# Window steps first with the compressed cells beside them, selected steps after: a hybrid trunk's sparse attention layer

## What is computed

```python
q = rms_norm(q) ; gate = sigmoid(gate)             # 3 gates per head
ck = rms_norm(compress(kc)) ; cv = compress(vc)    # 63 compressed cells per group
for each block of 128 queries:
    # 1. compressed: 63 cells
    s = q @ ck.T * scale + bias ; s = where(valid_c, s, NEG_INF)
    p_c = softmax(s) * any(valid_c) ; o_c = p_c @ cv
    # 2. selected: 8 of 16 blocks of 64 keys, chosen per group by the summed p_c
    imp = sum_over_heads(p_c) @ ov
    idx = top_k(where(valid & forced, FORCE_SCORE, where(valid, imp, -1)), 8)
    o_s = softmax(q @ k_sel.T * scale + bias) @ v_sel
    # 3. window: the last 512 keys
    o_w = softmax(q @ k_win.T * scale + bias + mask) @ v_win
o = gate0 * o_c + gate1 * o_s + gate2 * o_w
```

## Time and profile before

| | us |
|---|---|
| median of 3 runs | 2625.72 |
| lowest, highest | 2622.18, 2634.36 |
| the profiled execution | 2626.59 |
| its span (first to last instruction) | 2624.8 |
| TensorE busy in it | 2527.2 (96%) |
| VectorE, GpSimd, ScalarE busy | 1785.7, 1174.9, 1124.4 |
| mean granted TensorE clock | 0.979 |

### The profile page before, as it was taken

How to read it: one execution, slowest core, us unless ns; L and a number is a source line. 1 busy time by engine, 2 the same in 40 slices (tenths; PEclk the granted TensorE clock), 3 DMA queues, 4 the chain that set the end, 5 groups by cost and what they waited for, 6 DMA issues and landing times. The chain is left out here.

```text
span 2624.8 us, 37850 instructions
## 1 busy us (share of the span) xinstructions
PE 2527.2 (96%) x14000; PEld 2049.3 (78%) x14000; DVE 1785.7 (68%) x2826; ACT 1124.4 (43%) x2184; POOL 1174.9 (45%) x889
## 2 busy tenths in 40 slices
PE   8999889999999999999988999999999999999999
PEld 5777667888887878887876688888788888777887
DVE  6554755477678999853059567666546767899993
ACT  4626544253334434323135566666524333433431
POOL 5362666234445444442236444444633444444441
PEclk8999999999999999999987899999999999999999
DMA  4010003224343544230342423222132334354531
GB/s 168 33 49 33 1 1 117 93 81 161 140 169 134 188 170 146 83 127 32 102 118 65 129 59 100 54 54 54 56 125 79 146 135 170 109 209 149 175 125 65
DMA packets 90973, 275.76 MB, mean 105 GB/s; under 512 B 9879, under 2 KB 38935, under 8 KB 76135
## 3 DMA queue, kind: packets, MB, share of 16 engines
q1 hardware_dynamic: 87240, 255.18, 28.4%
q10 hardware_dynamic: 3552, 18.18, 1.8%
HBM read 197.50 MB, written 73.86 MB: 103 GB/s over the span
## 5 line engine op out<-in xcount | busy, mean ns | idle before, releaser
L1582 PE MATMUL ps<-U_hi,RH 128*128 128x512 f32 x912 | 356.7, 391 | 12.5 <-DVE H L905 4.8
L1586 PE MATMUL ps<-U_lo,RH 128*128 128x512 f32 x912 | 355.7, 390 | 0.0
L1587 PE MATMUL ps<-U_hi,RL 128*128 128x512 f32 x912 | 355.6, 390 | 0.0
L1040 POOL TENSOR_TENSOR RL<-RAW,RH 128x512 fp32r<-128x512 f32 x112 | 156.2, 1395 | 395.2 <-ACT RH L744 395.2
L744 ACT ACTIVATE RH<-RAW 128x512 fp32r<-128x512 f32 x280 | 175.5, 628 | 292.8 <-PE ps L1587 285.4
L1533 POOL TENSOR_SCALAR PX<-PX,rinv,GATE 128x640 f32<-128x640 f32 (+7 forms) x256 | 197.8, 783 | 209.0 <-DVE rinv L3303 209.0
L1582 PE MATMUL ps<-U_hi,W_hi 128*128 128x512 f32 (+2 forms) x656 | 261.9, 399 | 13.3 <-DVE U_lo L2805 10.7
L1582 PE MATMUL ps<-SH,RH 128*128 128x512 f32 x656 | 256.8, 392 | 8.2 <-DVE H L905 4.1
L1586 PE MATMUL ps<-U_lo,W_hi 128*128 128x512 f32 (+2 forms) x656 | 258.2, 394 | 0.0
L1587 PE MATMUL ps<-U_hi,W_lo 128*128 128x512 f32 (+2 forms) x656 | 258.1, 393 | 0.0
L1586 PE MATMUL ps<-SL,RH 128*128 128x512 f32 x656 | 255.9, 390 | 0.0
(11 more groups left out here) (390 smaller groups left out, 6005.9 us busy)
## 6 DMA issues: line engine op xcount, KB each, us to landing
W_raw<-in_pieces SPq DMA_DIRECT2D x30, 1024.0 KB, 5.1
RAW<-in_pieces SPq DMA_DIRECT2D x28, 1024.0 KB, 4.9
RAW<-in_pieces SPq DMA_DIRECT2D x56, 512.0 KB, 7.7
hid_d<-HOA SPq DMA_DIRECT2D x24, 1024.0 KB, 3.9
hid_d<-HOB SPq DMA_DIRECT2D x24, 768.0 KB, 5.4
RHA<-hid_d SPq DMA_DIRECT2D x12, 1024.0 KB, 5.1
RHB<-hid_d SPq DMA_DIRECT2D x12, 768.0 KB, 6.6
U_rawh<-hid_d SPq DMA_DIRECT2D x12, 768.0 KB, 4.8
```

The costliest lines, as they stand in the source:

```text
L1040: G_.tensor_tensor(ring(RL[i], n), quarter(n, (B22, B11)[i - 5]), ring(RH[i], n).bitcast(F32), ALU.subtract).then_inc(u_lop.sem, 1)
L1582: m = mm(o, a_hi, b_hi, start=first, stop=False, skip_group_check=again)
L1586: mm(o, a_hi, b_lo, start=False, stop=False, skip_group_check=again)
L1587: return mm(o, a_lo, b_hi, start=False, stop=last, skip_group_check=again)
```

## The change

Window and selected steps are no longer interleaved: `unit` gives all 64 window steps (eight pairs of eight) first, then all 64 selected ones. The cells' stage is gone as a stage. A cell is now half a pair (both heads, four query blocks), there are 16, and `cell(s, lag)` gives the cell whose part of that lag is due in step s: cell c has its scores at the end of step 4c + 4, maximum 1 step later, exponentials 2, sum 3, `share` 4, clamp, `add_up` and `gate_p` 5, its two turns 6 and 7 (ahead of the value products on TensorE, copied out ahead of the exponentials on ScalarE), its value product and output 9. Queries of pair p are turned in steps 8p - 6 and 8p - 5. The sums of group g are turned in step 32g + 41, chosen over the next six and the mask turned in 32g + 48 and 49.

Window scores are made of three products of 64 rows per head, straight from the pair's turned queries (one head in rows 0 to 63, the other in 64 to 127), the two heads alternating instruction by instruction. The selected ones are as before, with queries read back from memory.

Everything that TensorE turns (probabilities, queries, late keys, cells' scores, cells' probabilities, cells' value products, sums, masks) goes through banks 4 and 5 alternately by one list, `SEQ`; `room` waits until the last but one entry is emptied. GpSimd's two memsets of the mask rows come in steps 50 and 66, its splits of output weights in the last eight steps. The first engine queues are rewritten: window keys are turned first, and the last four key turns lie between the first two window scores and the loop. Loads and stores on SP follow the new order, and some tiles lie at other addresses.

The diff, cut to the order of the work, the banks, the window scores and the cells:

```diff
         SEL, WIN = 0, 1
-        STEPS = [x for k in range(NT) for x in ((SEL, NT - 1 - k), (WIN, NT - 1 - k))]
-        N_S = len(STEPS)
-        N_U = 2 * N_S
-        N_STEP = NH // 2 * N_S
+        N_PAIR = NH // 2
+        N_BR = N_PAIR * NT
+        N_STEP = 2 * N_BR
         N_ALL = 2 * N_STEP
+        N_CELL = 2 * N_PAIR
+        N_CHOOSE = 4 + 2 * NT
 
         def unit(U):
 
-            br, i = STEPS[U // 2 % N_S]
+            s = U // 2
+            br, i = (WIN if s < N_BR else SEL), NT - 1 - s % NT
             k0 = 0 if br == SEL else max(i - WB, 0)
-            return U // N_U * 2 + U % 2, br, i, k0, i + 1 - k0
+            return 2 * (s % N_BR // NT) + U % 2, br, i, k0, i + 1 - k0
...
+        def cell(s, lag):
+
+            c, r = divmod(s - 4 - lag, 4)
+            return c if r == 0 and 0 <= c < N_CELL else None
+
+        def query_of(s):
+
+            return [(p, h) for p in range(1, N_PAIR) for h in range(2) if s == 8 * p - 6 + h]
+
+        def imp_of(s, lag):
+
+            return [g for g in range(NG) if s == 32 * g + lag]
+
+        K_SEQ = (4, 5, 6, 7, 0, 1, 2, 3)
+        SEQ = [("q", 0, 0), ("q", 0, 1), ("g",), ("k", 2), ("k", 3), ("w2",)] + [("k", n) for n in range(4, 8)]
+        for s_ in range(N_STEP):
+            SEQ += [("p", 2 * s_, j) for j, _, _ in unit_chunks(2 * s_)]
+            SEQ += [("q", p, h) for p, h in query_of(s_)]
+            SEQ += [("ck",)] if s_ == 1 else []
+            SEQ += [("is", g) for g in imp_of(s_, 42)]
+            SEQ += [("t", cell(s_, 6 + e), e) for e in range(2) if cell(s_, 6 + e) is not None]
+            SEQ += [("p", 2 * s_ + 1, j) for j, _, _ in unit_chunks(2 * s_ + 1)]
+            SEQ += [("w", cell(s_, 9))] if cell(s_, 9) is not None else []
+            SEQ += [("it", g, h) for g in imp_of(s_, 41) for h in range(2)]
+            SEQ += [("im", g, h) for h in range(2) for g in imp_of(s_, 48 + h)]
+            SEQ += [("s", cell(s_, 0))] if cell(s_, 0) is not None else []
+        NO = {x: n for n, x in enumerate(SEQ)}
+        assert len(NO) == len(SEQ)
+
+        def made(*x):
+
+            return turned, NO[x] + 1
+
+        def rot(*x):
+
+            return 4 + NO[x] % 2
+
+        def emptied(n):
+
+            x = SEQ[n]
+            if x[0] == "p":
+                return (x_cpa, x_cpv)[x[1] % 2], CHUNKS[x[1] % 2][x[1]] + x[2] + 1
+            return {"q": lambda p, h: (t_lo, 2 * p + h + 1), "g": lambda: (c_sm, 1), "w2": lambda: (c_sm, 3),
+                    "k": lambda m: (k_lo, m + 1), "ck": lambda: (k_lo, 9), "s": lambda c: (e_add, c + 1),
+                    "t": lambda c, e: (e_tpev, 2 * c + e + 1), "w": lambda c: (e_o, c + 1),
+                    "it": lambda g, h: (i_tpev, 2 * g + h + 1), "is": lambda g: (i_dve, N_CHOOSE * g + 1),
+                    "im": lambda g, h: (i_mtrev, 2 * g + h + 1)}[x[0]](*x[1:])
...
+            def room(*x):
+
+                if NO[x] >= 2:
+                    pe.wait_ge(*emptied(NO[x] - 2))
+                return rot(*x)
+
...
+            def cmp_scores(c):
+
+                q, h = c // 2, c % 2
+                b = room("s", c)
+                pe.wait_ge(t_hi, 2 * q + 2)
+                pe.wait_ge(t_lo, 2 * q + 2)
+                if c == 0:
                     pe.wait_ge(k_lo, 9)
+                k_high, k_low = (t[:, 2 * q // HPG].rearrange("p a d -> p (a d)") for t in (CKH, CKL))
+                for i in range(4):
+                    j = 3 - i
+                    o, cols = ps[:, b, j * P:j * P + P], slice((4 * (1 - h) + i) * P, (4 * (1 - h) + i + 1) * P)
+                    mm(o, pair_high(q)[:, cols], k_high, start=True, stop=False)
+                    mm(o, pair_high(q)[:, cols], k_low, start=False, stop=False)
+                    m = mm(o, pair_low(q)[:, cols], k_high, start=False, stop=True)
+                m.then_inc(turned, 1)
+
+            def cmp_turn(c, e):
+
+                b = room("t", c, e)
+                pe.wait_ge(e_gated, c + 1)
+                for t in range(4):
+                    m = nc.tensor.transpose(ps[0:NCMP, b, t * P:t * P + P], PC[c % 4][:, 3 - t, e, :], ident)
+                m.then_inc(turned, 1)
+
+            def cmp_weigh(c):
+
+                b = room("w", c)
+                pe.wait_ge(e_tpev, 2 * c + 2)
+                for e in range(2):
+                    m = mm(ps[DK * e:DK * (e + 1), b, :].rearrange("p (t n) -> p t n", t=4), CV[:, 2 * (c // 2) // HPG, :], PTC[e],
+                           start=True, stop=True)
+                m.then_inc(turned, 1)
...
+            def scores(s):
+
+                hd, br, i, k0, nb = unit(2 * s)
+                g = hd // HPG
+                at_, end = first_col(nb), first_col(nb) + nb * P
+                parts = [(c0, c1) for c0, c1 in ((at_, min(HALF, end)), (HALF, end)) if c0 < c1]
+                if br == WIN:
+                    p = hd // 2
+                    if s % NT == 0:
+                        pe.wait_ge(t_hi, 2 * p + 2)
+                        pe.wait_ge(t_lo, 2 * p + 2)
+                    if s == 0:
+                        pe.wait_ge(k_hi, 4)
+                        pe.wait_ge(k_lo, 4)
+                    else:
+                        pe.wait_ge(x_max, 2 * s)
+                    n_left = [3 * len(parts)] * 2
+                    for q, keys in ((pair_high(p), KW2), (pair_high(p), KWS), (pair_low(p), KW2)):
+                        for c0, c1 in parts:
+                            for e in range(2):
+                                rows = slice(DK * e, DK * e + DK)
+                                n_left[e] -= 1
+                                m = mm(bank(2 * e, 2)[:, c0:c1], q[rows, i * P:(i + 1) * P],
+                                       keys[rows, g, k0 * P + c0 - at_:k0 * P + c1 - at_],
+                                       start=n_left[e] >= 2 * len(parts), stop=n_left[e] < len(parts))
+                                if n_left[e] == 0:
+                                    m.then_inc(x_qk, 1)
                 else:
-                    pe.wait_ge(e_add, 2 * q)
-                k_high, k_low = (t[:, 2 * q // HPG].rearrange("p a d -> p (a d)") for t in (CKH, CKL))
-                for i in range(NT):
-                    j = NT - 1 - i
-                    o, cols = ps[:, 2 + j // 4, j % 4 * P:j % 4 * P + P], slice(i * P, (i + 1) * P)
-                    mm(o, QHH[:, q % 2, cols], k_high, start=True, stop=False)
-                    mm(o, QHH[:, q % 2, cols], k_low, start=False, stop=False)
-                    m = mm(o, QLM[:, q % 2, cols], k_high, start=False, stop=True)
-                m.then_inc(e_qk, 2)
-
```

TensorE's order, then ScalarE's, VectorE's and GpSimd's:

```diff
+            pe.wait_ge(z_evac, Z1_UNITS + ZE)
+            compress(0)
+            turn_q(0, 0)
+            turn_q(0, 1)
+            turn_k(0)
+            turn_k(1)
+            compress(1)
+            turn_gates()
+            turn_k(2)
+            turn_k(3)
+            compress_out()
+            pe.wait_ge(const_in, 32)
+            scores(0)
+            turn_k(4)
+            turn_k(5)
+            scores(1)
+            turn_k(6)
+            turn_k(7)
             for s in range(N_STEP + 1):
-                for U in (2 * s + 4, 2 * s + 5):
-                    if U < N_ALL:
-                        scores(U)
+                if s + 2 < N_STEP:
+                    scores(s + 2)
                 if s < N_STEP:
                     turn_p(2 * s)
-                if s == 0:
-                    imp_mask(1)
+                for p, h in query_of(s):
+                    turn_q(p, h)
+                if s == 1:
+                    turn_ck()
+                for g in imp_of(s, 42):
+                    imp_sum(g)
+                for e in range(2):
+                    if cell(s, 6 + e) is not None:
+                        cmp_turn(cell(s, 6 + e), e)
                 if s:
                     weigh_p(s - 1)
                 if s < N_STEP:
                     turn_p(2 * s + 1)
+                if cell(s, 9) is not None:
+                    cmp_weigh(cell(s, 9))
+                for g in imp_of(s, 41):
+                    imp_turn(g, 0)
+                    imp_turn(g, 1)
+                for h in range(2):
...
+            expo(0)
+            expo(1)
+            key_high(4)
+            key_high(5)
             expo(2)
             expo(3)
-            act.wait_ge(i_sv, 16)
+            key_high(6)
+            key_high(7)
             for s in range(N_STEP + 1):
                 if s < N_STEP:
                     copy_p(2 * s)
-                if s == 0:
-                    mask_turned(1)
+                for p, h in query_of(s):
+                    q_high(p, h)
+                if s == 1:
+                    ck_high()
+                for e in range(2):
+                    if cell(s, 6 + e) is not None:
+                        cmp_turned(cell(s, 6 + e), e)
                 for U in (2 * s + 4, 2 * s + 5):
                     if U < N_ALL:
                         expo(U)
+                if cell(s, 2) is not None:
```

(63 more changed lines are left out.)

906 lines of the change are left out of this document (412 added, 494 removed).

## The result

| | before | after |
|---|---|---|
| median | 2627.43 (4 runs) | 2689.51 (4 runs) |
| lowest, highest | 2622.18, 2634.36 | 2687.45, 2695.51 |
| the profiled execution | 2626.59 | 2689.27 |
| its span | 2624.8 | 2687.5 |
| TensorE busy in it | 2527.2 | 2537.1 |

All times are microseconds. The ratio is 1.0226, with a 95% interval from 1.0201 to 1.025: the change makes the kernel slower by 62 us. The forecast was 2606 and the range ended at 2636, so the prediction was wrong in sign and in size, by 83 us.

The account below looks back on a forecast made before the run. Attention steps were taken as TensorE's own work, the cells ahead as a ring of waits. Terms summed to 11 + 251 + 26 + 219 + 7 + 3 = 517 us against 537.5, so 2626.6 - 20.5 = 2606; range 2576 to 2636.

Parts of the forecast that it names:

- term 5: Window pair's engine sums: VectorE 29.0 us, GpSimd 23, neither the bound on average against 31.4 + 3.3.
- the rival that should have held it: Window steps: VectorE bounds them, bank waits come on top, +15 to 20 us, 2623; chance 0.12.
- term 4: Window steps: turns wait for copies out of shared banks 4 and 5, 26 us in all, bounds 8 and 36.
- Term 1: Window scores: half-height products of two heads run side by side, 5.9 us a pair in place of 7.9.
- The slower rival: Window scores: row halves don't overlap, 6.0 us a pair more, 48 in all, 2646; chance 0.16.
- Terms 2 and 3: Window steps: more changes of the array's form, +2.4 us a pair; the cells placed there, +7.8 a pair.
- The sign for it: Window steps: weight-port "issue" waits, expected four a window step.
- Term 6: Selected steps: same instructions, 27.4 us a pair, 219 in all; waits for loads and memsets cost nothing.
- Term 7: Choosing the blocks: turns, sums and masks of both groups, 3.5 us of TensorE each, 7 in all.
- Term 8: Start of attention: first turn of probabilities near 1365, less 4 us of scores done early; net +11, between +5 and +13.
- Term 9: End: GpSimd's last split of output weights comes just ahead of the one-block step, +3 us (0 to 5).

Follow-up runs that it names:

- the first experiment: GpSimd's cell work one or two steps later in its queue, a cell's turns at lags 7 and 8, against the changed kernel: 2676.64 us, ratio 1.0195.
- the repaired kernel: Queries turned in steps 8p - 4 and 8p - 3, against the kernel with cells' items in the idle output bank and GpSimd later: 2608.6 us, ratio 0.992.

## Why the prediction was wrong

**What failed: term 5, and the rival that should have held it.** The prediction added up each engine's work over a pair, found GpSimd at 23 us against 34.7, and left it there. The sums are right (GpSimd 23.0 busy; VectorE's durations in a pair add up to 28.2, forecast 29.0). What no sum shows is that GpSimd's queue took from VectorE a result of the same iteration ahead of work that had been ready for an iteration. The order was in the diff. I went through TensorE's queue for what stands behind each new wait (term 4) and not through GpSimd's. This fault by itself is worth 38 us where the banks are separate (35 in the window half). Where they are shared it is 29 in the window half (330.6 to 301.8), and 16.5 if the cell's own turns come due too soon.

**Term 4: the right mechanism, too small.** With the queue out of the way, from shared banks to separate ones (301.8 to 267.7), and then to queries in better steps (261.5), is 40 us. 26 were taken, 36 was the upper bound. The three places that I had named are all there in the run with the queue out of the way: query turns at 0.64 a time (0.5 taken), cell scores 0.75 (0.6 taken), the cell's value product 0.75 (1.7 and 0.3 taken). Two were missing: the cell's own turns, 0.55 a time, and turns of probabilities that wait for VectorE, 0.8. The waits of scores for VectorE's minimum, 0.5 a time, come on top and are in the 40.

**How the window half adds up.** There are four kernels: both faults 330.6, only the banks 301.8, only GpSimd's queue 302.4, neither 267.7 (261.5 with the queries in better steps). Taking away either fault first saves 28 or 29 us, taking it away second 34 or 35. Of the 50 us over the forecast (330.6 against 280.5), 7 are left in the kernel with neither fault (261.5 against 254.5); the other 43 are the joint price of both faults, 69, less the 26 taken. How they divide between the two depends on which is taken first.

**The clock is part of the price.** From idle to time is a factor. Against the kernel with other banks, the kernel after has 37 us more idle time in its window half, but is 63 longer. It spends 51.2 us there at 1.2 GHz, with TensorE busy in 47.3 of them; the other kernel 6.8, all busy. Half of that busy time is what the lower clock adds, 23.7 and 3.4, so 20 of the 63; the other 6 are busy time at full clock. In its seven pairs from the second on the granted clock is between 0.88 and 0.96, while the same pairs of the other kernel have 1.00 but for one (0.91). Where I priced waits, I priced the wait alone; a granted clock of 1.0 from 1365 on was forecast.

But idle time alone doesn't say what the clock will cost. The kernel with shared banks and GpSimd out of the way had 41.8 us idle and the full clock throughout; the one with GpSimd early and other banks had 48.5 idle and 6.8 us at 1.2 GHz. In the first experiment waits of 1.44 us on TensorE were followed by a lower clock in some pairs and not in others. And in the kernel with the queries in better steps the clock was at 1.2 GHz from 1558.6 to 1568.8, with no wait of TensorE in the nine us ahead; half of these 10.2 us, busy throughout, are 5 of the 7 that it lies over the forecast. What makes the clock fall is not shown here. So 20 us of the kernel after's loss are a lower clock that no term of the sum could have given.

**Term 1, right.** 1.07 us for five blocks (0.95 to 1.0 was forecast, 1.27 before by the earlier trace rows), the two heads side by side. The Trainium skill (TensorEngine Tiling (Array Packing), Tiling Modes) says that such tiles work in parallel, and the trace agrees. The slower rival, which alone stood between the range and a slower result, was not what happened. Its price stays untested: with one head's products behind the other's, five blocks took 1.48 and not 1.9, but the two heads still overlapped in part.

**Terms 2 and 3, right together.** The steady pair of the kernel with queries in better steps takes 32.6, of which 1.3 idle: 31.3, where 31.4 was the forecast for scores, changes of form and cells. A change of form is not measured by itself, so one of them too large and another too small would look the same. The sign for it was four "issue" waits of the weight port a window step; from 1400 to 1650 there are 138 ahead of turns, scores and value products (18.6, 11.7 and 7.4 us), three a step.

**Term 6: right in the work, wrong in "cost nothing".** Steady selected pairs take 28.0 (27.4). The loads of heads 6 and 7 were said to be issued ten steps ahead. In fact they stood on SyncE's queue behind a store that waits for the last step of choosing, and cost 11.5 us; I had looked at when the loads were due, and not at what was ahead of them. The rest of the excess lies in the first two selected pairs, 35 us each in place of 28. Of these 14 us, 3.5 are the second choice, which the sum had there, and some 5 are the last cells (four groups of turns and three value products, at 0.46 and 0.93 by the earlier trace rows): no loss, but work that the sum had put into the window half, so that the window half's own excess is larger by as much. Of the 6 left, 4 are idle time over a steady pair's (2.9 and 2.6 against 0.6), nearly all of it cells', sums' and masks' items and probabilities waiting for copies out of banks 4 and 5: term 4 again, where the sum had nothing for it. 2 stay unexplained.

**Term 7** stands in that. **Term 8**: the first turn of probabilities came at 1363.6 as forecast (near 1365), but the first value product only at 1370.4:

```profile
1363.62 1.33 PE L2192 MATMUL ps<-cs,PX 128*128 128x128 f32 x5 [3.17 <-POOL PX L1532]
1365.52 1.30 PE L2192 MATMUL ps<-cs,PX 128*128 128x128 f32 x5 [0.56 <-ACT PT L2681]
1366.75 0.90 PE L2167 MATMUL ps<-KW,QHH 64*128 64x384 f32 x4
```

Turns at 1.3 us in place of 0.77 show the lower clock (1362.2 to 1369.0) at a wait of 3.17 us, and the bank's waits (0.56 and 0.58) come on top: these 6.8 us would be some 3.2 at full clock without waits. The forecast's 1361 was the 1365 of the first turn less 4 for scores done early. So of the 9.4 us, 3.6 are lost to clock and banks, 1.4 were gained at the first turn, and 7.2 are no loss: the 4 credited, and 3.2 of work that lies ahead of the first value product. They come back at the end, where the last selected pair needs no more scores for a next one (25.3 us with its 3.7 of idle time, against 28.0), so the selected half's own excess is larger by about as much. **Term 9**: 3.7 us of idle ahead of the last step's first turn (1946.65), released by GpSimd, forecast 3.

**The chances.** The forecast's mechanism for most terms was right. That the repaired kernel measures 2608.6 against 2606 is luck all the same: the 2606 have 26 us of waits for banks that this kernel mostly doesn't have, and without them the forecast would be 2580. The range only held errors in the size of named terms. Its weakness was that three queues with new orders (GpSimd, SyncE, TensorE's banks) had one rival between them.

## What to carry to other kernels

When side work is woven into a pipelined loop, write for every engine which iteration of its neighbours it really works on; an engine that runs ahead must take side work from an earlier iteration, or its wait holds up the main work that is long ready. Sums of busy time per stage can't show this: go through each in-order queue, SyncE's too, and ask of each new wait what behind it was ready. And where stalls on TensorE recur, look at the granted clock beside them: here 37 us of them came with 20 more from a lower clock, while 42 in another kernel came with none.

## What the runs showed of the hardware

- Products of 64 rows on the two halves of the array ran side by side in the faster 32-bit form: five blocks of two heads, 12 products of 384 or 256 columns, took 1.07 us in three groups of four, 0.39, 0.30 and 0.38 us apart.
- The second head's products didn't wait for the first head's to end when they stood behind them in program order; they started beside the first head's third (1.48 us in place of 1.07).
- In the window half of the kernel after, the clock fell to 1.2 GHz eleven times, in most pairs close to waits of 1.67 to 3.0 us on TensorE (1.67 at 1492.0, the lower clock from 1491.9 to 1498.7), and the granted clock of steady pairs was 0.88. In other kernels 24 waits of 1.0 to 3.0 us went with one fall, 41.8 us of shorter waits with none, and one fall (1558.6 to 1568.8) came with no wait in the nine us ahead.
- Five turns took 1.33 us at 1.2 GHz and 0.77 at 2.4.
